# Expert weights loaded four tiles at a time, as runs of 32 KB per partition, in a two-block transformer kernel on one core

## The chip, the cores and the metric

The kernel runs on one core of one Trainium2 chip, with the other seven idle. The metric is the device time of one launch in microseconds (us). All arithmetic is float32 (some operands are split in a high and a low float32r part). Five engines have programs of their own, written out by hand, and meet at semaphores: PE (TensorE, the matrix products), DVE (VectorE), ACT (ScalarE), POOL (GpSimd) and SP (SyncE), which here only issues DMAs.

## The reference

Two blocks over 256 tokens of width 1024. The first block is a gated recurrent mixer followed by a mixture of experts; the second is another mixer with a gated output. The change touches the mixture of experts and, by one term, the router ahead of it:

```
def moe_expert_choice(h, router_w, w_gate, w_up, w_down):
    cap = CAPACITY_FACTOR * T // N_EXPERTS            # 2 * 256 // 16 = 32 tokens for each expert
    aff = softmax(h @ router_w)
    gate, idx = top_k(swapaxes(aff, 1, 2), cap)       # each of the 16 experts picks its 32 tokens
    xs = h[idx]
    hid = silu(xs @ w_gate) * (xs @ w_up)             # w_gate, w_up: 16 x 1024 x 2048
    ye = (hid @ w_down) * gate                        # w_down: 16 x 2048 x 1024
    return zeros.at[idx].add(ye)
```

The three weight tensors are 16 x 3 x 8 MB = 384 MB (MB here is 1024 x 1024 bytes; in the profile's rows it is 1,000,000). They are read once.

## The kernel before

**Tiles.** The expert weights are cut into 24 x 16 = 384 tiles of 1 MB (128 partitions x 8 KB), numbered `t = 0 .. 383`: for each expert `x`, tiles `24x .. 24x+7` are `w_gate` (`wg`), the next eight `w_up` (`wu`), the last eight `w_down` (`wd`). One DMA loads a pair of tiles, `t` and `t+1`, 2 MB: each partition receives one run of 16 KB that is contiguous in HBM (two rows of `wg`/`wu`, or four rows of `wd`). Because partition `p` holds rows `2p, 2p+1`, the activations that meet a tile are gathered with a stride (`H2k[..., k % 2 :: 2]`), and the inner values `hid` are turned by four transposes of `hid[:, c::4]`.

**Buffers.** SBUF is cut into slots of 8 KB per partition. A slot number names a place: 0 to 4 are the five slots of the dense weights (`wslot0` to `wslot4`), 5 and up are the pages of a zone (`zpair(i)` is page `i`), `EXTRA = 25` is a pair of pages of its own (page 17), and `APART = 26` is a mark, not a place: its two tiles go to `wslot4` and to page 15, by two DMAs of 1 MB. The table `PAIRS` gives the place of each pair in order of time. The first ten pairs (`t = 0 .. 19`) fill empty places; the sixth to tenth are issued when the last dense weights free them. From `t = 20` on each pair waits until PE has used the tiles that lay in its place; `before(t)` looks up which tile that is, and SP waits for `p_exp.at("tile", before(t))`. In the steady state nine pairs are in turn, so a pair is asked for when 16 tiles (16 MB) are still outstanding.

**SP's order.** SP issues every weight DMA in the order of the program, and a wait on SP holds back all that stands behind it. Ahead of the experts stand the loads of the first block's dense weights; behind the last expert pair stand those of the second block, `weights(n)`.

**PE's order.** At the end of the first block's dense products come four small products of `ffs` with parts of the identity (line 1918), which bring two vectors into the layout of the gathered activations. Then the output projection, the router, and, interleaved with the products of expert 0, the gathering of activations (`gather_first`, `gather`). `up(x, m, b)` runs the eight tiles of `wg` (m = 0) or `wu` (m = 1): it waits for a pair at every second tile, runs four products per tile (line 2113) and signals `p_exp("tile", t)`. Then `hid` is turned (line 2132, signal `hidT`), and the `wd` tiles follow (line 2147), two per turn of the loop. The last pair, `t = 382`, comes as two DMAs of 1 MB.

Of the kernel before, what the change touches and what calls it, by code (L numbers as in the profile page):

```python
# [64 lines left out]
def program(nc, a, out):  # L65
    ctx = ExitStack()
    with ctx:
# [124 lines left out]
        WH2 = [put(f"whj{i}", 2048, page(p), FR) for i, p in enumerate((14, 15, 6))]  # L192
# [10 lines left out]
        c2, c2l = both("c2", 2048, page(0))  # L203
# [101 lines left out]
        zpair = lambda i: BASE + i  # L305
# [5 lines left out]
        tile_page = lambda t: PAIRS[t // 2]  # L311
        pairs = {r: put(f"pair{r}", 2 * SLOT, page(17) if r == EXTRA else slots_at + r * SLOT if r < BASE else page(r - BASE)) for r in set(PAIRS) - {APART}}
        apart = (slots[4], put("apart", SLOT, page(15)))

        def tile_at_page(t):
            return apart[t % 2] if tile_page(t) == APART else pairs[tile_page(t)][:, t % 2 * SLOT:t % 2 * SLOT + SLOT]

        last_tile = lambda r: max(2 * i + 1 for i in range(12 * NE) if PAIRS[i] == r)
# [6 lines left out]
        def expert_src(t):  # L325
            e_, m, k = t // 24, t % 24 // 8, t % 8
            if m == 2:
                return a["wd"][e_, 256 * k:256 * k + 512, :].rearrange("(p c) n -> p (c n)", c=4)
            return a["wu" if m else "wg"][e_, 128 * k:128 * k + 256, :].rearrange("(p c) n -> p (c n)", c=2)
# [50 lines left out]
        def sync(e):  # L380
# [39 lines left out]
            def experts(t):  # L420
                if tile_page(t) == APART:
                    e.dma_start(apart[0], expert_src(t)[:, 0:SLOT]).then_inc(*landed[APART]())
                    e.dma_start(apart[1], expert_src(t)[:, SLOT:2 * SLOT]).then_inc(*landed[APART]("expert", t))
                    return
                if t == 24 * NE - 2:

                    e.dma_start(pairs[tile_page(t)][:, 0:SLOT], expert_src(t)[:, 0:SLOT]).then_inc(*l_last())
                    e.dma_start(pairs[tile_page(t)][:, SLOT:2 * SLOT], expert_src(t)[:, SLOT:2 * SLOT]).then_inc(*landed[tile_page(t)]("expert", t + 1))
                    return
                e.dma_start(pairs[tile_page(t)], expert_src(t)).then_inc(*landed[tile_page(t)]("expert", t))  # L430
# [31 lines left out]
            for t in range(10, 24 * NE, 2):  # L462
# [11 lines left out]
                elif before(t) is not None:  # L474
                    e.wait_ge(*p_exp.at("tile", before(t)))
                elif tile_page(t) == zpair(12):
                    e.wait_ge(*a_moe.at("xs", 1, 7))
                experts(t)

            for n in range(SECOND, NT):  # L480
                if n < SECOND + 4:
                    e.wait_ge(*p_exp.at("tile", last_tile(tile_slot(n) // 2 * 2)))
                elif n == SECOND + 4:
                    e.wait_ge(*p_exp.at("tile", max(i for i in range(24 * NE) if tile_page(i) == APART)))
# [3 lines left out]
                if n == SECOND + BASE - 1:  # L488
                    e.wait_ge(*p_exp.at("tile", last_tile(zpair(10))))
# [8 lines left out]
        def scalar(e):  # L498
# [220 lines left out]
            for k in range(8):  # L719
                if k == 7:  # L720
                    e.wait_ge(*p_exp.at("tile", 2 * PAIRS.index(EXTRA) + 1))
                    pp_left(0)
# [892 lines left out]
        def gpsimd(e):  # L1615
# [34 lines left out]
            e.wait_ge(*p_exp.at("tile", last_tile(zpair(0))))  # L1650
# [3 lines left out]
        def tensor(e):  # L1654
# [261 lines left out]
            for b_ in range(2):  # L1916
# [501 lines left out]
```

## Time and profile before

| | |
|---|---|
| time, median of 3 runs (lowest, highest) | 1550.55 us (1549.97, 1551.77) |
| time of the profiled execution | 1551.3 us |
| its span in the trace | 1549.5 us |
| granted TensorE clock, mean | 0.89 of full |
| PE busy | 1207.3 us (78%) |
| PE weight loads busy | 730.7 us (47%) |
| DVE / ACT / POOL busy | 562.5 / 423.9 / 29.9 us |
| DMA moved | 520.90 MB, 336 GB/s over the span |

The profiled execution's time is 1.8 us above its span. The page of the profile cuts the span into 40 slices of 38.7 us. The first eight (to about 310 us) are the first block's dense part, the next 23 (to about 1200 us) the experts, the last eight the second block. A "pair" in the rows is a pair of expert tiles, `wslot` a slot of dense weights, `xs` the gathered activations, `B` a bank of PSUM.

### The profile page before, as it was taken

To read this page: it belongs to the slowest core of one execution; us is meant where nothing else is said; L and a number is where in the kernel's file an instruction comes from. 1 tells how busy PE (TensorE), PEld (TensorE's weight loads), DVE (VectorE), ACT (ScalarE), POOL (GpSimd) and SP (SyncE) were. 2 spreads that over 40 slices of the span, in tenths; PEclk is the share of its full clock that TensorE was granted. 3 is DMA by queue.
4 is the path that set the end of the run, shared out by engine and by line. 5 is a ranking of instruction groups with operands and counts; after the bars stand their busy time and mean duration, and the time that the engine had idled before them with its cause. 6 is when DMAs were issued, how large, how long until landed. Compare 5 with 4: busy or idle time off the path is not lost.

```text
span 1549.5 us, 18615 instructions
## 1 busy us (share of the span) xinstructions
PE 1207.3 (78%) x8122; PEld 730.7 (47%) x8122; DVE 562.5 (36%) x829; ACT 423.9 (27%) x553; POOL 29.9 (2%) x36
## 2 busy tenths in 40 slices
PE   4999999999656656656666656656666899999998
PEld 1878899943111212111111111211211589999997
DVE  3887776511101101101101101101101497777566
ACT  2865646232000000000000000000000454467545
POOL 0012000000000000000000000000000000000000
PEclk9999999999778878778867888878778999999999
DMA  9546859699999999999999999999999855555551
GB/s 364 207 156 229 301 209 337 223 403 429 426 428 428 428 428 427 428 428 426 428 428 427 427 428 428 427 427 429 428 427 428 327 164 163 163 183 184 184 186 55
DMA packets 118719, 520.90 MB, mean 336 GB/s; under 512 B 7264, under 2 KB 85088, under 8 KB 90736
## 3 DMA queue, kind: packets, MB, share of 16 engines
q1 hardware_dynamic: 118496, 519.64, 83.9%
q8 instruction: 64, 1.05, 0.3%
q10 hardware_dynamic: 144, 0.09, 0.0%
q14 instruction: 15, 0.12, 0.0%
HBM read 518.66 MB, written 1.05 MB: 335 GB/s over the span
## 4 chain that ended last, share of the span: by engine, by line
DMA 53%; PE 43%; DVE 2%; ACT 1%; SPq 1%; issue 0%; DVEq 0%
DMA pair<-in_wu 27%; PE B L1697 16%; DMA pair<-in_wd 12%; DMA pair<-in_wg 11%; PE B L1705 6%; PE B L2113 4%; PE B L1709 3%; DMA wslot<-in_w_in 2%; PE B L1824 2%; PE B L2147 1%; PE B L1675 1%; PE B L1812 1%; PE B L1827 1%; DMA wslot<-in_w_out 1%; DMA wslot<-in_ada_w 1%; PE B L2074 0%
## 5 line engine op out<-in xcount | busy, mean ns | idle before, releaser
L2113 PE MATMUL B<-pair,xs 128*32 128x512 f32 x2048 | 323.1, 758 | 193.0 <-DMA pair<-in_wu 121.5
L2113 PEld LDWEIGHTS B<-pair,xs 128*32 128x32 f32 x2048 | 63.2, 124 | 413.0 <-issue 180.1
L2147 PE MATMUL B<-pair,hidT 128*32 128x512 f32 x1008 | 167.9, 799 | 102.1 <-DMA pair<-in_wd 96.6
L1697 PE MATMUL B<-hnh,whj 128*128 128x256 f32 x488 | 138.1, 283 | 0.0
L1697 PE MATMUL B<-hnh,wslot_r 128*128 128x256 f32 x488 | 137.6, 282 | 0.0
L1697 PE MATMUL B<-hn_r,whj 128*128 128x256 f32 x488 | 137.1, 281 | 0.0
L2147 PEld LDWEIGHTS B<-pair,hidT 128*32 128x32 f32 x1008 | 32.3, 128 | 218.6 <-DMA pair<-in_wd 143.2
L955 DVE TENSOR_TENSOR wslot_r<-wslot,whj 128x2048 fp32r<-128x2048 f32 x52 | 118.9, 2289 | 31.3 <-ACT whj L509 31.3
L509 ACT ACTIVATE whj<-wslot 128x2048 fp32r<-128x2048 f32 x51 | 97.2, 1913 | 87.6 <-PE B L1697 82.0
L1289 DVE SCALAR_TENSOR_TENSOR x<-B,mod,x 128x256 f32<-128x256 f32 x128 | 56.0, 480 | 163.5 <-PE B L2092 163.3
L1320 DVE COPY ye<-B 128x512 f32<-128x512 f32 x15 | 10.4, 692 | 269.6 <-PE B L2147 269.6
L1309 DVE TENSOR_TENSOR hid<-sgm,B 128x512 f32<-128x512 f32 x16 | 11.0, 688 | 260.8 <-PE B L2113 260.8
L1697 PEld LDWEIGHTS B<-hnh,wslot_r 128*128 128x128 f32 x488 | 93.6, 192 | 0.0
L1697 PEld LDWEIGHTS B<-hn_r,whj 128*128 128x128 f32 x488 | 91.8, 188 | 0.1
L1697 PEld LDWEIGHTS B<-hnh,whj 128*128 128x128 f32 x488 | 91.7, 188 | 0.1
L736 ACT ACTIVATE hidT<-B 128x512 f32<-128x512 f32 x16 | 9.6, 597 | 271.1 <-PE B L2132 271.1
L730 ACT ACTIVATE gt<-B 128x256 f32<-128x256 f32 x16 | 6.1, 383 | 273.4 <-PE B L2124 273.4
L745 ACT ACTIVATE ye<-B 128x512 f32<-128x512 f32 x15 | 9.0, 597 | 247.7 <-PE B L2147 247.7
L955 DVE TENSOR_TENSOR wslot_r<-wslot,whi 128x2048 fp32r<-128x2048 f32 x29 | 66.3, 2286 | 13.0 <-ACT whi L509 10.7
L1705 PE MATMUL B<-hh,whi 128*128 128x256 f32 (+1 forms) x256 | 71.0, 308 | 0.0
L1705 PE MATMUL B<-h_r,whi 128*128 128x256 f32 (+1 forms) x256 | 69.6, 303 | 0.0
L2092 PE MATMUL B<-gt,ye 128*128 128x256 f32 x256 | 68.4, 413 | 1.5
(505 smaller groups left out, 1908.8 us busy)
## 6 DMA issues: line engine op xcount, KB each, us to landing
pair<-in_wg SPq DMA_DIRECT2D x64, 2048.0 KB, 41.2
pair<-in_wu SPq DMA_DIRECT2D x64, 2048.0 KB, 40.9
pair<-in_wd SPq DMA_DIRECT2D x62, 2048.0 KB, 40.9
wslot<-in_w_in SPq DMA_DIRECT2D x58, 1024.0 KB, 5.2
aslot<-in_ada_w SPq DMA_DIRECT2D x20, 1024.0 KB, 7.2
wslot<-in_ada_w SPq DMA_DIRECT2D x4, 1024.0 KB, 9.1
wslot<-in_w_out SPq DMA_DIRECT2D x4, 1024.0 KB, 8.5
wslot<-in_wa SPq DMA_DIRECT2D x4, 1024.0 KB, 5.1
```

Source lines behind the costliest of these rows:

```text
L509: e.activation(hi_(n), raw(n), ACT.Copy).then_inc(*a_hi(n))
L955: e.tensor_tensor(lo_(n), raw(n), hi_(n).bitcast(F32), ALU.subtract).then_inc(*v_lo(n))
L1289: e.scalar_tensor_tensor(XX[:, db, :], B[scat_bank(x, db // 2)][:, 256 * (db % 2):256 * (db % 2) + 256], mod[:, 40 + db, 0:1], XX[:, db, : ...
L1675: mm = e.matmul(B[0][32 * j:32 * j + 32, :], csil[:, k, :], slots[s][:, 512 * j:512 * j + 512], start=k == 0, stop=k == 7)
L1697: mm = e.matmul(ps, w[:, k, :], x(k), start=k == 0 and j == 0, stop=k == kn - 1 and j == 2)
L1705: e.matmul(ps, l, r, start=k == 0 and j == 0, stop=False)
L1709: mm = e.matmul(ps, l, r, start=False, stop=k == kn - 1)
L1812: mm = e.matmul(B[4 + j][:, half(h)], K0[:, h, half(j)], Q0[:, h, half(i)], start=True, stop=True)
L1824: e.matmul(ps, x[:, 4 * half_k + k, tk], wh[:, k, :], start=half_k == 0 and k == 0 and x is ah, stop=False)
L2092: mm = e.matmul(B[b][:, 256 * j:256 * j + 256], YE[:, half(db)], Gt, start=True, stop=True)
L2113: mm = e.matmul(B[b][32 * j:32 * j + 32, :], XS[x // 8][:, k, 32 * (x % 8):32 * (x % 8) + 32], tile_at_page(t)[:, 512 * j:512 * j + 512], ...
L2147: mm = e.matmul(B[3 + db][32 * r:32 * r + 32, :], hidT[:, 128 * c + 32 * j:128 * c + 32 * j + 32], v2(tile_at_page(t + c // 2))[:, c % 2, ...
```

## The change

- From `t = 28` on, four tiles are loaded by one DMA of 4 MB: each partition receives one run of 32 KB contiguous in HBM. There are 88 such loads (`t = 28 .. 379`), in turn over four places: slots 0 to 3, and pages 8, 0 and 4 of the zone (each four pages wide).
- The first 14 loads stay pairs, in the same places as before, and the last two (`t = 380`, `382`) are pairs too. A pair is now half of a run of 32 KB, so partition `p` holds rows `4p .. 4p+3` of `wg`/`wu`, or `8p .. 8p+7` of `wd`, spread over four tiles. The gathering strides become 4 in place of 2 (same number of products).
- `hid` is turned by sixteen products with parts of the identity (64 columns each) in place of four transposes; the products of `ffs` become 16 in place of 4.
- The table is now `LOADS`, a list of (first tile, number of tiles, place). `before(load)` now looks for earlier loads whose slots, counted as `place .. place + number - 1`, overlap those of the load.
- The third high-part buffer of the second block (`WH2`) and the buffer `c2` exchange pages 6 and 0.

The core of the diff:

```
-        TURN = [zpair(2), zpair(4), zpair(12), zpair(0), zpair(6), 0, 2, zpair(8), zpair(10)]
         EXTRA = BASE + MORE + AUX
         APART = EXTRA + 1
-        PAIRS = TURN[:2] + [EXTRA] + TURN[3:] + [APART] + 2 * (TURN[:2] + TURN[3:])
-        PAIRS += [TURN[i % 9] for i in range(12 * NE - len(PAIRS))]
+        LOADS = [(2 * i, 2, r) for i, r in enumerate((zone_at(2), zone_at(4), EXTRA, zone_at(0), zone_at(6), 0, 2, zone_at(8), zone_at(10), APART,
+                                                      zone_at(2), zone_at(4), zone_at(0), zone_at(6)))]
+        for t in range(28, 24 * NE, 4):
+            r = zone_at(8) if t == 24 * NE - 4 else (0, zone_at(8), zone_at(0), zone_at(4))[(t - 28) // 4 % 4]
+            LOADS += [(t, 2, r), (t + 2, 2, r + 2)] if t == 24 * NE - 4 else [(t, 4, r)]
...
-        def before(t):
-
-            earlier = [i for i in range(t // 2) if PAIRS[i] == PAIRS[t // 2]]
-            return 2 * earlier[-1] + 1 if earlier else None
+        in_slot = lambda s, load: load[2] <= s < load[2] + load[1]
+        def before(load):
+
+            t0, n, r = load
+            earlier = [x[0] + x[1] - 1 for x in LOADS if x[0] < t0 and any(in_slot(s, x) for s in range(r, r + n))]
+            return max(earlier) if earlier else None
...
-            for t in range(10, 24 * NE, 2):
+            for load in LOADS[5:]:
+                t = load[0]
...
-                elif before(t) is not None:
-                    e.wait_ge(*p_exp.at("tile", before(t)))
-                elif tile_page(t) == zpair(12):
-                    e.wait_ge(*a_moe.at("xs", 1, 7))
+                elif before(load) is not None:
+                    e.wait_ge(*p_exp.at("tile", before(load)))
                 experts(t)
...
-            for b_ in range(2):
-                for hf in range(2):
-                    mm = e.matmul(B[4][64 * hf:64 * hf + 64, 0:16].rearrange("p (m q b) -> p b m q", m=2, b=2)[:, b_], ident[:, b_::2],
-                                  ffs.rearrange("p (m q h) -> p h m q", m=2, h=2)[:, hf], start=True, stop=True)
+            for b_ in range(4):
+                for hf in range(4):
+                    mm = e.matmul(B[4][32 * hf:32 * hf + 32, 0:16].rearrange("p (m q b) -> p b m q", m=2, b=4)[:, b_], ident[:, b_::4],
+                                  ffs.rearrange("p (m q h) -> p h m q", m=2, h=4)[:, hf], start=True, stop=True)
...
-                for c in range(4):
-                    mm = e.transpose(B[2][:, half(c)], hid[:, c::4], ident)
+                for c in range(8):
+                    for q in range(2):
+                        mm = e.matmul(B[2][64 * q:64 * q + 64, 64 * c:64 * c + 64].rearrange("p (j s) -> p j s", j=2), hid[:, c::8],
+                                      ident.rearrange("p (j q s) -> p q j s", q=2, s=32)[:, q], start=True, stop=True)
```

**SP at the start of the experts, before.** The rows are SP's DMAs in order: `pair_198` holds `t = 12`, `pair_203` `t = 14`, `pair_204` `t = 16`; `wslot_57` and `apart` together hold `t = 18` and `19` (the APART load); then `t = 20, 22, 24, 26, 28, 30`.

```order
73 L430 DMA pair_198<-in_wu 128x4096 [waits pe_proj]
74 L430 DMA pair_203<-in_wu 128x4096 [waits pe_proj]
75 L430 DMA pair_204<-in_wd 128x4096
76 L422 DMA wslot_57<-in_wd 128x2048
77 L423 DMA apart<-in_wd 128x2048
78 L430 DMA pair_200<-in_wd 128x4096 [waits pe_expert]
79 L430 DMA pair_201<-in_wd 128x4096 [waits pe_expert]
80 L430 DMA pair_199<-in_wg 128x4096 [waits pe_expert]
81 L430 DMA pair_202<-in_wg 128x4096 [waits pe_expert]
82 L430 DMA pair_197<-in_wg 128x4096 [waits pe_expert]
83 L430 DMA pair_198<-in_wg 128x4096 [waits pe_expert]
```

**The same place of SP in the changed kernel.** Row 82 is the first load of four tiles (`t = 28`).

```order
73 L443 DMA pair_203<-in_wu 128x4096 [waits pe_proj]
74 L443 DMA pair_298<-in_wu 128x4096 [waits pe_proj]
75 L443 DMA pair_299<-in_wd 128x4096
76 L435 DMA wslot_57<-in_wd 128x2048 [waits pe_expert]
77 L436 DMA apart<-in_wd 128x2048
78 L443 DMA pair_206<-in_wd 128x4096 [waits pe_expert]
79 L443 DMA pair_207<-in_wd 128x4096 [waits pe_expert]
80 L443 DMA pair_208<-in_wg 128x4096 [waits pe_expert]
81 L443 DMA pair_209<-in_wg 128x4096 [waits pe_expert]
82 L443 DMA four_294<-in_wg 128x8192 [waits pe_expert]
83 L443 DMA four_295<-in_wu 128x8192 [waits pe_expert]
```

No load has moved in the order, but the first DMA of the APART load (row 76) has gained a wait for a tile that PE has used, and from row 82 on one DMA stands where two stood. By the new `before`, the APART load has place 26 and two slots, 26 and 27; the EXTRA load (`t = 4`) has place 25 and two slots, 25 and 26; they overlap at 26, so the wait is for tile 5.

**PE ahead of the output projection, before.** `ffs` is the small vector pair, `hh` and `bf_r` are operands of dense products.

```order
935 L1709 MATMUL B<-hh,wslot_r 128x256 x7
936 L1918 MATMUL B<-ffs,ident 64x8 [waits dve_mid,dve_left_bank]
937 L1918 MATMUL B<-ffs,ident 64x8 x3
938 L1923 MATMUL B<-wrbsum,ones 128x16 [waits dve_left_bank]
939 L1705 MATMUL B<-bf_r,whi_98 128x256 [waits act_hi,dve_clamped,dve_h]
```

**The same place of PE in the changed kernel.**

```order
935 L1721 MATMUL B<-hh,wslot_r 128x256 x7
936 L1930 MATMUL B<-ffs,ident 32x4 [waits dve_mid,dve_left_bank]
937 L1930 MATMUL B<-ffs,ident 32x4 x15
938 L1935 MATMUL B<-wrbsum,ones 128x16 [waits dve_left_bank]
939 L1717 MATMUL B<-bf_r,whi_98 128x256 [waits act_hi,dve_clamped,dve_h]
```

Twelve small products are added in front of the projections. The turning of `hid` grows in the same way, from four products of 128x128 to sixteen of 64x64 for each expert, at the same place of PE's order.

## Rows read from the trace of the kernel before

**Rows 1.** The page: the span in 40 slices, DMA share, GB/s and PE's clock.

```profile
PEclk9999999999778878778867888878778999999999
DMA  9546859699999999999999999999999855555551
GB/s 364 207 156 229 301 209 337 223 403 429 426 428 428 428 428 427 428 428 426 428 428 427 427 428 428 427 427 429 428 427 428 327 164 163 163 183 184 184 186 55
```

**Rows 2.** The page: the chain that ended last, by line.

```profile
DMA pair<-in_wu 27%; PE B L1697 16%; DMA pair<-in_wd 12%; DMA pair<-in_wg 11%; PE B L1705 6%; PE B L2113 4%; PE B L1709 3%; DMA wslot<-in_w_in 2%; PE B L1824 2%; PE B L2147 1%; PE B L1675 1%; PE B L1812 1%; PE B L1827 1%; DMA wslot<-in_w_ou
```

**Rows 3.** Waits of PE from 400 to 1180 us: total us, times, longest.

```profile
PE B L2113 <- DMA pair<-in_wu: 113.0, 52, 3.1
PE B L2147 <- DMA pair<-in_wd: 88.4, 46, 3.0
PE B L2113 <- DMA pair<-in_wg: 66.2, 35, 3.2
```

**Rows 4.** DMA queues from 420 to 1180 us: packets, MB, share of 16 engines.

```profile
DMA packets 22324, 325.10 MB, mean 428 GB/s; under 512 B 2480, under 2 KB 2480, under 8 KB 2480
q1 hardware_dynamic: 22298, 324.71, 100.5%
q8 instruction: 22, 0.36, 0.2%
pair<-in_wu SPq DMA_DIRECT2D x52, 2048.0 KB, 41.3
```

**Rows 5.** DMA queues from 1300 to 1500 us (the second block's dense weights).

```profile
DMA packets 35507, 36.04 MB, mean 180 GB/s; under 512 B 544, under 2 KB 35490, under 8 KB 35490
q1 hardware_dynamic: 35490, 35.79, 56.2%
wslot<-in_w_in SPq DMA_DIRECT2D x20, 1024.0 KB, 5.2
```

**Rows 6.** SP's issues in order of time, from 300 us: start, us, what.

```profile
303.34 0.43 SPq L430 DMA_DIRECT2D pair<-in_wd  x1
303.81 0.43 SPq L422 DMA_DIRECT2D wslot<-in_wd  x1
304.29 0.74 SPq L423 DMA_DIRECT2D apart<-in_wd  x1
318.36 4.53 SPq L430 DMA_DIRECT2D pair<-in_wd  x2
329.19 12.24 SPq L430 DMA_DIRECT2D pair<-in_wg  x4
```

**Rows 7.** DMA issues at 304.29 and at 329.19: KB, us to landing.

```profile
apart<-in_wd SPq DMA_DIRECT2D x1, 1024.0 KB, 17.7
pair<-in_wg SPq DMA_DIRECT2D x1, 2048.0 KB, 10.1
```

**Rows 8.** PE in order of time from 315 us: tiles 0, 1, 5.

```profile
315.65 1.07 PE L2113 MATMUL B<-pair,xs 128*32 128x512 f32 x8
...
317.23 1.06 PE L2113 MATMUL B<-pair,xs 128*32 128x512 f32 x8
...
325.62 1.07 PE L2113 MATMUL B<-pair,xs 128*32 128x512 f32 x8
```

**Rows 9.** Windows in us: busy time of PE, PEld, DVE, ACT, POOL, PEclk, DMA share, GB/s.

```profile
318.00:320.00 2.00, 2.00 (x18) 0.93 (x14) 0.00 (x0) 0.38 (x1) 0.00 (x0) 1.00 0.87 369
320.00:322.00 2.00, 2.00 (x18) 0.93 (x14) 0.00 (x0) 0.38 (x1) 0.00 (x0) 1.00 0.95 352
330.00:332.00 2.00, 2.00 (x14) 0.85 (x12) 0.00 (x0) 1.94 (x4) 0.20 (x1) 1.00 0.93 303
332.00:334.00 2.00, 2.00 (x14) 0.85 (x12) 0.69 (x1) 0.83 (x2) 0.00 (x0) 1.00 0.92 303
```

**Rows 10.** PE in order of time from 250.5 us.

```profile
250.63 0.41 PE L1918 MATMUL B<-ffs,ident 128*64 128x8 f32 x8
250.98 0.39 PE L1923 MATMUL B<-wrbsum,ones 128*128 128x16 f32 x2
```

More of the change, by code:

```diff
@@ L189, in program @@
         gkh_ = put("gkh", 128, lbv_at + 128, FR)
-        WH2 = [put(f"whj{i}", 2048, page(p), FR) for i, p in enumerate((14, 15, 6))]
+        WH2 = [put(f"whj{i}", 2048, page(p), FR) for i, p in enumerate((14, 15, 0))]
         YH, YL = v8(put("yh", 2048, page(7), FR)), v8(put("yl", 2048, page(8), FR))
@@ L202, in program @@
         hn, hnl = both("hn", 2048, page(13))
-        c2, c2l = both("c2", 2048, page(0))
+        c2, c2l = both("c2", 2048, page(6))
         PT2, mg2l = both("PT2", 2048, page(1))
@@ L313, in program @@
+        load_of = {t: load for load in LOADS for t in range(load[0], load[0] + load[1])}
+        tile_page = lambda t: load_of[t][2]
+        homes = {(n, r): put(("pair" if n == 2 else "four") + str(r), n * SLOT, page(17) if r == EXTRA else slots_at + r * SLOT if r < BASE else page(r - BASE))
+                 for _, n, r in LOADS if r != APART}
         apart = (slots[4], put("apart", SLOT, page(15)))
         def tile_at_page(t):
-            return apart[t % 2] if tile_page(t) == APART else pairs[tile_page(t)][:, t % 2 * SLOT:t % 2 * SLOT + SLOT]
@@ L318, in program, with last_tile @@
-        last_tile = lambda r: max(2 * i + 1 for i in range(12 * NE) if PAIRS[i] == r)
-        def before(t):
-            earlier = [i for i in range(t // 2) if PAIRS[i] == PAIRS[t // 2]]
-            return 2 * earlier[-1] + 1 if earlier else None
-        def expert_src(t):
+            t0, n, r = load_of[t]
+            return apart[t - t0] if r == APART else homes[n, r][:, (t - t0) * SLOT:(t - t0 + 1) * SLOT]
+        in_slot = lambda s, load: load[2] <= s < load[2] + load[1]
+        def last_tile(s):
+            return max(load[0] + load[1] - 1 for load in LOADS if in_slot(s, load))
@@ L420, in experts @@
             def experts(t):
-                if tile_page(t) == APART:
-                    e.dma_start(apart[0], expert_src(t)[:, 0:SLOT]).then_inc(*landed[APART]())
-                    e.dma_start(apart[1], expert_src(t)[:, SLOT:2 * SLOT]).then_inc(*landed[APART]("expert", t))
+                n, r = load_of[t][1:]
+                if r == APART:
+                    e.dma_start(apart[0], expert_src(t, 2)[:, 0:SLOT]).then_inc(*landed[APART]())
+                    e.dma_start(apart[1], expert_src(t, 2)[:, SLOT:2 * SLOT]).then_inc(*landed[APART]("expert", t))
                     return
                 if t == 24 * NE - 2:
-                    e.dma_start(pairs[tile_page(t)][:, 0:SLOT], expert_src(t)[:, 0:SLOT]).then_inc(*l_last())
-                    e.dma_start(pairs[tile_page(t)][:, SLOT:2 * SLOT], expert_src(t)[:, SLOT:2 * SLOT]).then_inc(*landed[tile_page(t)]("expert", t + 1))
+                    e.dma_start(homes[n, r][:, 0:SLOT], expert_src(t, 2)[:, 0:SLOT]).then_inc(*l_last())
+                    e.dma_start(homes[n, r][:, SLOT:2 * SLOT], expert_src(t, 2)[:, SLOT:2 * SLOT]).then_inc(*landed[r]("expert", t + 1))
                     return
-                e.dma_start(pairs[tile_page(t)], expert_src(t)).then_inc(*landed[tile_page(t)]("expert", t))
+                e.dma_start(homes[n, r], expert_src(t, n)).then_inc(*landed[r]("expert", t))
             def later(j):
@@ L481, in sync @@
                 if n < SECOND + 4:
-                    e.wait_ge(*p_exp.at("tile", last_tile(tile_slot(n) // 2 * 2)))
+                    e.wait_ge(*p_exp.at("tile", last_tile(tile_slot(n))))
                 elif n == SECOND + 4:
-                    e.wait_ge(*p_exp.at("tile", max(i for i in range(24 * NE) if tile_page(i) == APART)))
+                    e.wait_ge(*p_exp.at("tile", last_tile(APART)))
                 else:
@@ L488, in sync @@
                 if n == SECOND + BASE - 1:
-                    e.wait_ge(*p_exp.at("tile", last_tile(zpair(10))))
+                    e.wait_ge(*p_exp.at("tile", last_tile(zone_at(11))))
                     e.dma_start(wgk[0:16, :], a["w_gk2"]).then_inc(*l_gk())
@@ L720, in scalar @@
                 if k == 7:
-                    e.wait_ge(*p_exp.at("tile", 2 * PAIRS.index(EXTRA) + 1))
+                    e.wait_ge(*p_exp.at("tile", last_tile(EXTRA)))
                     pp_left(0)
```

24 lines of the change are left out of this document (13 added, 11 removed).

## Prediction

> **What bounds the kernel now.** I read the 40 slices of the page first. From about 350 to 1200 us every slice has a DMA share of 9 tenths or more and 426 to 429 GB/s, while PE's granted clock falls to 0.7 to 0.8 [rows 1]: in this stretch TensorE stands at its lower level (1.2 GHz) for part of the time and at 2.4 GHz for the rest, because it has too little to do. The chain of work that ended last gives half of the span to the three weight tensors (27 + 12 + 11%) [rows 2]. PE's waits say the same from the other side: between 400 and 1180 us PE waits 113.0 + 88.4 + 66.2 = 267.6 us for expert tiles [rows 3]. So the expert stage ends when its 384 MB have come through the DMA queues. Two things can move that end: how fast the stream runs, and how long it stands still. Work of PE counts only where a load waits for it.
>
> **The stream: what a longer run is worth.** At 428 GB/s [rows 4] a pair of 2,097,152 bytes takes 4.900 us. Each of the 16 DMA engines carries 8 runs of 16 KB and one small packet for the semaphore in that time. How much of it goes with the packet and not with the bytes? The queue view of this stretch has 22,298 - 2,480 = 19,818 large packets; 100.5% of 16 engines for 760 us is 12,221 us, so 616.7 ns each [rows 4]. The second block has 35,490 - 544 = 34,946 packets of 1 KB in 56.2% of 16 x 200 us, so 51.5 ns each [rows 5]. Between 1 KB and 16 KB a KB costs (616.7 - 51.5) / 15 = 37.7 ns. The bytes of a pair therefore take 8 x 16 x 37.7 ns = 4.823 us. Of the 4.900 us some 0.005 us are instruction loads (0.36 of 325.1 MB [rows 4]), and 0.072 us are left that come once per DMA of 8 runs, whatever their length. A load of four tiles pays them once for 4 MB: 9.72 us in place of 9.79. Over the 88 loads that is 88 x 0.072 = 6.3 us saved. The bounds: the intercept of a small packet is 51.5 - 37.7 = 13.8 ns, which over 8 x 88 = 704 packets fewer per engine makes 9.7 us; and nothing, if a run of 32 KB goes out as two packets. I take 6.3, since it comes from the rate of this very stretch. The trace has no packet of 32 KB, so all of this is an estimate from the rows at 1 and 16 KB.
>
> The Trainium skill, "DMA: Bandwidth & Descriptors", section "Why small descriptors are slow", puts the cost inside an engine at about 3 cycles per packet, next to one cycle for every 32 bytes. By it a packet's own part would be some 3.5 ns and the saving 2.5 us; the rows give 0.072 / 8 = 9 ns, so the trace does not agree, though it has no run of 32 KB to decide it. That is a rival below.
>
> **The stream: a hole at its start.** The listing of SP shows the term that weighs most. In the changed kernel the first DMA of the APART load (t = 18) waits for PE to finish tile 5. The place of this load needs no such wait: EXTRA (25, two slots) and APART (26, a mark) overlap only by their numbers. Before, t = 16, 18 and 19 were issued at 303.34, 303.81 and 304.29 us, one right behind the other [rows 6], and tile 19 landed 17.7 us later, at 322.0 [rows 7]; as its 4.9 us of data end there, those of t = 18 began at 317.1. At 318.36, when tile 1 was done, t = 20 followed, and the stream hardly broke [rows 6, 9]. Tile 5 is done only at 325.62 + 1.07 = 326.7 us [rows 8]. SP is in order, so t = 20, 22, 24 stand behind the waiting load although tiles 1 and 3 are long used.
>
> PE itself arrives a little later. The four products of ffs take 0.35 us from their start to the next product's (250.63 to 250.98) [rows 10]; sixteen take, by the same 0.09 us, 1.4 us, some of it a fixed drain. PE has hardly a gap there, so I add 0.8 us (bounds 0 and 1.05). Tile 5 then ends at 327.5, and the load is issued at 327.55. From issue to first data: a tile of 1 MB with 1 KB runs lands after 5.2 us, of which 64 packets x 51.5 ns = 3.3 us are data [rows 5], so about 2.0 us with its completion. The data of t = 18 start at about 329.55 in place of 317.1: 12.5 us later. Between, nothing is in the queue.
>
> Not all of this reaches the end, for the stream of before also had small dips: at 318 to 322 us (369 and 352 GB/s) and at 330 to 334 (303 twice) [rows 9] it lost 0.3 + 0.4 + 1.2 = 1.8 us against 428. With loads asked for in time behind the hole these vanish, which leaves 10.7. Measured at a later load: t = 24 landed at 329.19 + 10.1 = 339.3 [rows 6, 7]; now it lands four pairs behind 329.55, at 349.15, 9.9 us later, but a landing is set by the slowest of 16 engines, and a hole lets all start level. I take 11.6, the middle of 10.7 and 12.5; the bounds are 9.9 and 12.5.
>
> Behind the hole nothing else is late. PE needs (325.62 - 317.23) / 4 = 2.1 us per tile here [rows 8], so tile 13, for which the first load of four (t = 28) waits, is done near 344, while the pairs up to t = 26 keep the queue full until 354. Tile 17 (for t = 32) is done near 353, before t = 28 ends at 364; tile 25 near 370, before t = 32 ends at 374. In the steady state a load of four is asked for when 12 tiles are outstanding in place of 16, so 29 us of data in place of 39 (before, a pair landed 41.3 us after its issue [rows 4]). PE would have to be more than 27 us behind for the queue to run dry, and it is the one that waits.
>
> **What costs nothing.** The turning of hid: twelve more small products per expert, at the 0.09 us of those of ffs [rows 10] 1.1 us each time, up to double at the lower clock. The waits of PE for tiles (267.6 us) [rows 3] hide them; if that cover were gone they would cost 17 us or more. The gathering keeps its number of products. At the end of the stage the last tiles come as pair, single, single, as before; the dense weights behind them have the same places. The wait of wgk for tile 383 stands behind dense tiles that are issued later than that tile's use. The exchanged pages 6 and 0 are both free by then.
>
> **Sum.** 11.6 (hole, with the 0.8 of PE in it) - 6.3 (88 loads) = +5.3 us. Against the profiled execution's 1551.3 us that is 1556.6. The median of the three runs is 0.75 us lower, 1550.55, so I predict 1555.9 us. A measurement of this kernel can tell about 0.2%, 3.1 us, from no change.
>
> **The rivals.**
> - *The two nearly cancel.* A packet costs nearly the 13.8 ns of the intercept (9 us saved) and the hole costs its lower bound (9.9 to 11): 10.9 - 8.9 = +2, 1552.6 us. For it: the intercept itself; against it: the rate of the stretch leaves no room for 13.8 ns. 0.16.
> - *The longer run gives back little.* By the 3 cycles of the page above: 11.6 - 2.5 = +9.1, 1559.7 us. The 9 ns from the rate speak against it, the lack of any row at 32 KB for it. 0.09.
> - *The run is cut into packets of 16 KB.* Then only the hole is left: +11.6, 1562.2 us. The runs of 16 KB went out whole (19,818 packets carry the bytes of as many runs [rows 4]), which speaks against. 0.05.
> - *The loads of four run slower*, from how 16 engines spread over HBM when a partition's rows lie 32 KB apart, or from a queue that runs dry. Each per cent on 88 x 9.8 us is 8.6 us: 1551.3 + 11.6 + 8.6 - 0.7 = 1570.8. It takes over from the forecast once a load of four takes more than 9.79 us. 0.04.
> - *Faster than before.* A long run moves its bytes faster than 37.7 ns per KB, so that the stream gives back more than the hole: it needs 11.6 + 3.1 = 14.7 us, 0.167 us per load, a load of four in under 9.63 us (436 GB/s). At 438 GB/s a load takes 9.58 us, 88 x 0.21 = 18.5 us are saved, and the time is 1550.55 + 11.6 - 18.5 = 1543.7 us. No slice of the page's long stretch is over 429. 0.07.
>
> **How the numbers follow.** The forecast has 0.59, with a range of its own of 1553.7 to 1558.7 (hole 10.7 to 12.5, saving 4.4 to 7.5). Slower by over 0.2%: forecast, little given back, cut, slower loads, 0.59 + 0.09 + 0.05 + 0.04 = 0.77. Within 0.2%: 0.16. Faster: 0.07. The range of 1551.5 to 1562.0 takes in the forecast, most of the near-cancelling case, and the case of little given back; it leaves out the faster case and the two slowest.
>
> **What the profile of the changed kernel would show.** If the hole is right: SP's issue of t = 18 right behind tile 5, near 327.5 us, with t = 20 and 22 within 1 us behind it, and windows of 0 GB/s between about 317 and 329 us. If the price of a packet is right: packets of 32 KB, 88 x 128 = 11,264 fewer in all, and 431 GB/s in the long stretch. At 429 the page's 3 cycles hold; at 428 or below the runs are cut or slowed. Waits of PE for hid's turning should not appear on the chain that ended last. The prediction is wrong above all if the hole is shorter (tile 5 earlier, or the queue still full), or if the stream's rate moves by more than 1%.

## The result, and the profile of the changed kernel

The changed kernel takes 1558.93 us in the median (1557.54 to 1560.2, 4 runs), the kernel before in the same series 1551.12 (1549.97 to 1551.77, 4 runs). The ratio is 1.0051, with a 95% interval of 1.0034 to 1.0068: slower by 7.8 us, between 5.3 and 10.5. The profiled execution took 1558.16 us with a span of 1556.4, against 1551.3 and 1549.5 before, 6.9 us more. The granted clock is 0.895 in the mean.

The page of the changed kernel, its 40 slices (the span is 1556.4 us, a slice 38.9):

```profile
PEclk9999999999888788878878787877797999999999
DMA  9646768659999999999999999999999855455551
GB/s 363 217 156 232 284 231 331 233 240 432 432 431 433 431 432 430 430 431 432 430 431 430 431 432 430 432 431 431 431 432 430 331 168 171 155 183 185 184 188 55
```

Against [rows 1] two things have changed. The ninth slice, 311 to 350 us, has fallen from 403 to 240 GB/s. The long stretch behind it has risen from 426 to 429 up to 430 to 433. These are the two terms of the prediction: a hole, and a faster stream.

**The hole.** SP's DMAs in order of time, changed kernel, from 302 us (start, us, what):

```profile
302.67 0.43 SPq L443 DMA_DIRECT2D pair<-in_wd  x1
329.16 0.33 SPq L435 DMA_DIRECT2D wslot<-in_wd  x1
329.53 0.43 SPq L436 DMA_DIRECT2D apart<-in_wd  x1
330.35 1.02 SPq L443 DMA_DIRECT2D pair<-in_wd  x2
332.07 4.91 SPq L443 DMA_DIRECT2D pair<-in_wg  x2
345.48 0.33 SPq L443 DMA_DIRECT2D four<-in_wg  x1
```

The APART load (`t = 18`) stands 26.5 us behind `t = 16`, where it stood 0.5 us behind it [rows 6]. With it go `t = 20` and `22` (the row with 1.02 us), `t = 24` and `26` (4.91 us). Windows of the changed kernel (columns as in [rows 9]):

```profile
314.00:316.00 2.00, 2.00 (x13) 1.86 (x16) 0.48 (x2) 0.52 (x2) 0.00 (x0) 1.00 0.00 0
316.00:328.00 12.00, 12.00 (x68) 6.57 (x60) 0.00 (x0) 2.12 (x6) 0.00 (x0) 1.00 0.01 1
328.00:330.00 2.00, 2.00 (x13) 1.13 (x12) 0.00 (x0) 0.60 (x2) 0.62 (x1) 1.00 0.00 0
330.00:332.00 2.00, 2.00 (x18) 0.52 (x19) 0.00 (x0) 1.81 (x4) 0.00 (x0) 1.00 0.94 262
332.00:352.00 20.00, 19.12 (x121) 10.74 (x120) 2.06 (x3) 6.59 (x13) 0.62 (x1) 1.00 1.01 431
```

For 16 us, from 314 to 330, nothing moves. PE is busy the whole time: it works on what it has, and the queue is empty beside it. The first DMA behind the hole and `t = 24`, from issue to landing (KB, us):

```profile
wslot<-in_wd SPq DMA_DIRECT2D x1, 1024.0 KB, 4.8
pair<-in_wg SPq DMA_DIRECT2D x1, 2048.0 KB, 20.5
```

`t = 24` lands at 332.07 + 20.5 = 352.6, before at 339.3 [rows 6, 7]: 13.2 us later. Why the wait lasts to 329.1 and not to 327.5 stands in PE's order of time, around tile 0, tile 1 and tile 5:

```profile
315.75 1.07 PE L2125 MATMUL B<-pair,xs 128*32 128x512 f32 x8
316.75 1.12 PE L2076 MATMUL B<-pick,h2k 128*128 128x32 f32 x4
317.80 1.06 PE L2125 MATMUL B<-pair,xs 128*32 128x512 f32 x8
...
328.04 1.06 PE L2125 MATMUL B<-pair,xs 128*32 128x512 f32 x8
```

Tile 0 starts 0.1 us later than before, tile 5 2.4 us later. From tile 1 on a tile takes (328.04 - 317.80) / 4 = 2.56 us in place of 2.1 [rows 8]. Between two tiles stand the products that gather activations. Grouped by line and form (busy us, mean ns), they read their weights (`H2k`, a step of four floats) so:

```profile
L2086 PEld LDWEIGHTS B<-pick,h2k 128*128 128x128 f32 x64 | 16.4, 325 | 12.6 <-ACT xs L725 9.2 <-issue 3.2
L2076 PEld LDWEIGHTS B<-pick,h2k 128*128 128x128 f32 x32 | 8.0, 325 | 5.0 <-issue 3.4 <-ACT xs L720 1.7
```

Before, with a step of two floats, the second of these groups read:

```profile
L2064 PEld LDWEIGHTS B<-pick,h2k 128*128 128x128 f32 x32 | 4.3, 196 | 5.0 <-issue 3.4 <-ACT xs L708 1.7
```

The same number of products, but 325 ns for each weight load in place of 196: four of them between two tiles are 0.52 us, about the difference of the pace.

**The stream.** Queues of the changed kernel from 420 to 1180 us (packets, MB, share of 16 engines):

```profile
DMA packets 11257, 327.51 MB, mean 431 GB/s; under 512 B 1248, under 2 KB 1248, under 8 KB 1248
q1 hardware_dynamic: 11230, 327.10, 100.1%
```

The runs of 32 KB went out whole: 11,230 - 1,248 = 9,982 large packets in 100.1% of 16 x 760 us, 1.219 us each, where two of 16 KB took 1.233 [rows 4]. A load of four, 4,194,304 bytes, takes 9.73 us at 431 GB/s and 9.80 at 428: 0.07 us on each of 88, or 6.0 us. The rounding of either rate alone is worth up to 1 us there. With the rates unrounded (327.51 and 325.10 MB in 760 us) the two loads take 9.733 and 9.805 us, and the 88 give 6.3 us.

At the end of the stage, PE's rows of the last `wd` tiles:

```profile
1217.20 5.34 PE L2162 MATMUL B<-four,hidT 128*32 128x512 f32 x32 [1.44 <-DMA four<-in_wd]
1223.56 1.92 PE L2162 MATMUL B<-pair,hidT 128*32 128x512 f32 x16
1226.50 1.92 PE L2162 MATMUL B<-pair,hidT 128*32 128x512 f32 x16
```

The last tile lands at 1226.99 us in the trace, and landed at 1220.42 before: 6.6 us later, so of the 13.2 at `t = 24` the stream has given back 6.6 by then, about what its rate says. The last 0.3 us of the 6.9 arise behind it: PE comes to the last pair at 1226.50 us and runs all its 16 products after that, while before it had run the first eight already when the last tile landed, and had only this row left:

```profile
1220.47 1.07 PE L2147 MATMUL B<-pair,hidT 128*32 128x512 f32 x8 [1.14 <-DMA pair<-in_wd]
```

**Turning `hid`.** The turning before and now, grouped by form:

```profile
L2132 PE MATMUL B<-ident,hid 128*128 128x128 f32 x64 | 12.3, 317 | 14.1 <-DVE hid L1309 14.1
```

```profile
L2145 PE MATMUL B<-ident,hid 128*64 128x64 f32 x512 | 34.5, 287 | 14.2 <-DVE hid L1321 14.2
```

34.5 us busy for 12.3. No sign of it reaches the end: PE still waits for tiles between 400 and 1180 us (total us, times, longest), 266.9 us in all for 267.6 before [rows 3]:

```profile
PE B L2125 <- DMA four<-in_wu: 121.8, 26, 5.8
PE B L2162 <- DMA four<-in_wd: 87.9, 22, 7.3
PE B L2125 <- DMA four<-in_wg: 57.2, 20, 6.3
```

### The profile page after: what moved, and what is told of

Its sections match the earlier page's. It is cut to its first block, busy times and chain, and to the rows that moved or that the text cites. A ratio compares the mean times of both kernels' runs of the same rounds, so it can differ in the third digit from the quotient of the medians.

```text
span 1556.4 us, 19468 instructions
## 1 busy us (share of the span) xinstructions
PE 1216.9 (78%) x8594; PEld 779.3 (50%) x8594; DVE 562.3 (36%) x829; ACT 424.1 (27%) x553; POOL 29.8 (2%) x36
## 4 chain that ended last, share of the span: by engine, by line
DMA 48%; PE 48%; DVE 2%; ACT 1%; SPq 1%; issue 1%; DVEq 0%
DMA four<-in_wu 17%; PE B L1709 16%; DMA four<-in_wd 15%; DMA four<-in_wg 15%; PE B L2125 7%; PE B L1717 6%; PE B L1721 3%; PE B L2162 3%; PE B L1836 2%; PE B L1687 1%; PE B L1824 1%; PE B L1839 1%; PE B L2086 1%; DMA wslot<-in_w_out 1%; DMA wslot<-in_ada_w 1%
## 5 line engine op out<-in xcount | busy, mean ns | idle before, releaser
L2125 PE MATMUL B<-four,xs 128*32 128x512 f32 x1888 | 304.3, 800 | 197.3 <-DMA four<-in_wu 135.4
L2125 PEld LDWEIGHTS B<-four,xs 128*32 128x32 f32 x1888 | 75.3, 140 | 401.5 <-issue 323.9
L2162 PE MATMUL B<-four,hidT 128*32 128x512 f32 x928 | 142.5, 769 | 93.5 <-DMA four<-in_wd 89.3
L2162 PEld LDWEIGHTS B<-four,hidT 128*32 128x32 f32 x928 | 35.2, 136 | 188.6 <-DMA four<-in_wd 87.2
L967 DVE TENSOR_TENSOR wslot_r<-wslot,whi 128x2048 fp32r<-128x2048 f32 x29 | 66.2, 2284 | 12.9 <-ACT whi L521 10.5
L2104 PE MATMUL B<-gt,ye 128*128 128x256 f32 x256 | 63.4, 391 | 1.6
## 6 DMA issues: line engine op xcount, KB each, us to landing
pair<-in_wg SPq DMA_DIRECT2D x6, 2048.0 KB, 11.6
```

The source lines that it names most:

```text
L967: e.tensor_tensor(lo_(n), raw(n), hi_(n).bitcast(F32), ALU.subtract).then_inc(*v_lo(n))
L2104: mm = e.matmul(B[b][:, 256 * j:256 * j + 256], YE[:, half(db)], Gt, start=True, stop=True)
L2125: mm = e.matmul(B[b][32 * j:32 * j + 32, :], XS[x // 8][:, k, 32 * (x % 8):32 * (x % 8) + 32], tile_at_page(t)[:, 512 * j:512 * j + 512], ...
L2162: mm = e.matmul(B[3 + db][32 * r:32 * r + 32, :], hidT[:, 256 * (j % 2) + 64 * c + 32 * (j // 2):256 * (j % 2) + 64 * c + 32 * (j // 2) + 32],
```

## Experiments

Theory after the result: three terms. The wait of `t = 18` costs the hole; the gathering's longer weight loads put PE behind, which lengthens the wait; the cost of a packet comes back on 88 loads. Rivals: that the hole alone explains the loss; that the cost falls once per DMA and not once per packet; that loads of four cost something by themselves.

The median of the kernel before was 1551.06 us in the series of the first four runs below, 1551.37 in that of the next four, and 1551.2 in that of the last two. Each run is compared with the one of its own series.

### The APART load gets a number of its own

```
-        APART = EXTRA + 1
+        APART = EXTRA + 2
-        landed = [signal(f"landed{i}", 16) for i in range(BASE + MORE + AUX + 2)]
+        landed = [signal(f"landed{i}", 16) for i in range(BASE + MORE + AUX + 3)]
```

> The changed kernel with the APART load given a number of its own, so that it waits for no tile. Theory: the wait for tile 5 made the hole of 13 us (stream of t = 18 from 331.0 instead of 317.1 us), and PE's pace of 2.56 us per tile (2.1 before; weight reads of the gathering 325 ns instead of 196) asks for t = 20, 24 and t = 28 too late. Then the dry times move to these: about 1.5 us before t = 20, 3.4 before t = 24, 3.6 before t = 28, the first load of four lands near 357 instead of 365.3 (first engine), and the kernel is about 8 us faster than the changed one: 1551 us, even with before. Rival A: PE's pace does not matter; then only the hole goes, 13 us faster, 1546 us. Rival B: the loss lies in the later stage; then the time stays near 1559 us.

Measured: 1553.79 us (1549.73 to 1556.29, 10 runs), ratio 1.0016 [1.0005, 1.0026]. That is 2.7 us above the kernel before, in place of 7.8. So 5.1 us of the loss go with the wait, less than the hole that could be read in the trace and less than the 8 that were expected. SP issues `t = 18` right behind `t = 16` again, but now other holes appear. SP's issues and windows of this run:

```profile
319.63 6.84 SPq L443 DMA_DIRECT2D pair<-in_wd  x2
334.16 4.91 SPq L443 DMA_DIRECT2D pair<-in_wg  x2
347.57 0.33 SPq L443 DMA_DIRECT2D four<-in_wg  x1
```

```profile
318.00:320.00 2.00, 2.00 (x11) 0.51 (x3) 0.00 (x0) 0.12 (x1) 0.00 (x0) 0.50 0.22 90
320.00:322.00 2.00, 2.00 (x9) 1.13 (x13) 0.00 (x0) 0.38 (x1) 0.00 (x0) 0.50 0.69 180
332.00:334.00 2.00, 2.00 (x18) 0.55 (x17) 0.00 (x0) 1.71 (x4) 0.00 (x0) 1.00 0.25 107
346.00:348.00 2.00, 2.00 (x13) 0.96 (x13) 0.00 (x0) 0.54 (x1) 0.00 (x0) 1.00 0.02 8
```

`t = 24` is issued at 334.16, 5.0 us later than before [rows 6]. The queue runs dry before `t = 20`, before `t = 24` and before the first load of four, because PE is late with the tiles that they wait for. In the changed kernel these waits were hidden in the large hole. Part of the lateness in this run is the clock: 0.50, the level of 1.2 GHz, between 318 and 322 us. How much of the 2.7 us is the clock's, the run doesn't tell: its ten times go from 1549.73 to 1556.29 us, and the traced one, 1555.09, is among the longer ones.

### The kernel before, with the wait alone

```
+                elif t == 18:
+                    e.wait_ge(*p_exp.at("tile", 5))
```

> The kernel before with one wait added: the load of t = 18 waits for tile 5. Theory: t = 18 is issued near 326.8 us, its data start near 328.8 instead of 317.1, the dips at 320 and 330 us go; t = 26 lands 9.5 to 11 us later than before, and the kernel takes 1561 us. Rival: the stream makes the hole good later (a stage that is not bound by DMA), then under 1554 us.

Measured: 1561.03 us (1559.66 to 1561.78, 4 runs), ratio 1.0065 [1.0048, 1.0082]. The wait alone costs 10.0 us by the medians and 10.5 by the spans of the two traces (1560.0 and 1549.5), inside the 9.9 to 12.5 of the prediction and in its lower part. SP issues `t = 18` as soon as tile 5 is done, and the stream stands from about 316 us on:

```profile
326.27 0.33 SPq L422 DMA_DIRECT2D wslot<-in_wd  x1
```

```profile
316.00:326.00 10.00, 10.00 (x72) 4.42 (x68) 0.00 (x0) 1.89 (x5) 0.61 (x1) 1.00 0.01 2
```

That is 2.9 us earlier than in the changed kernel. The rest of that kernel's hole is not the wait's.

### Each four as two DMAs of 16 KB runs

On top of the own number:

```
+                if n == 4:
+                    e.dma_start(homes[n, r][:, 0:2 * SLOT], expert_src(t, 4)[:, 0:2 * SLOT]).then_inc(*landed[r]())
+                    e.dma_start(homes[n, r][:, 2 * SLOT:4 * SLOT], expert_src(t, 4)[:, 2 * SLOT:4 * SLOT]).then_inc(*landed[r]("expert", t))
+                    return
```

> As e1, but each load of four goes out as two DMAs of 2 MB with runs of 16 KB, one right behind the other, same places and waits. Theory (a cost of 8 to 9 ns once per packet): 428 GB/s again in the long stretch, 0.07 us more per load of four, 6 us slower than e1: 1557 us. Rival (the rate comes from fewer waits or from the addresses, not from the run): 431 GB/s and the time of e1.

Measured: 1558.82 us (1556.95 to 1563.25, 4 runs), ratio 1.0058 [1.0039, 1.0077], 5.0 us above the run with the own number. The time alone proves little, since the clock fell in this run's trace too (0.50 from 320 to 328 us, in the longest of its four executions); the rate of the long stretch is the evidence. The queues, 420 to 1180 us:

```profile
DMA packets 22323, 325.05 MB, mean 428 GB/s; under 512 B 2482, under 2 KB 2482, under 8 KB 2482
```

Everything but the length of the run and the number of DMAs is as it was, and the rate is back at 428. So neither the layout nor the places nor the waits of the loads of four make the stream fast; the length of the run or the smaller number of DMAs does.

### Each four as two DMAs of 64 partitions

To keep the 32 KB runs and double the DMAs, each four was cut by partitions:

```
+                    e.dma_start(homes[n, r][0:64, :], expert_src(t, 4)[0:64, :]).then_inc(*landed[r]())
+                    e.dma_start(homes[n, r][64:128, :], expert_src(t, 4)[64:128, :]).then_inc(*landed[r]("expert", t))
```

> As e1, but each load of four goes out as two DMAs, partitions 0 to 63 and 64 to 127, with runs of 32 KB. The number of DMAs doubles as in e3, the packets stay at 32 KB. Theory (cost per packet, a semaphore packet about 9 ns): at most 1 us slower than e1, 430.5 to 431 GB/s. Rival (cost per DMA): 6 us slower, 428 GB/s, as e3.

Measured: 2447.26 us (2445.01 to 2449.91, 4 runs), ratio 1.5785 [1.5761, 1.5808]. The queues, 420 to 1180 us:

```profile
DMA packets 6097, 159.70 MB, mean 210 GB/s; under 512 B 1216, under 2 KB 1216, under 8 KB 1216
q1 hardware_dynamic: 6083, 159.49, 100.2%
```

The experiment doesn't answer its question. It shows something else: (6,083 - 1,216) = 4,867 packets of 32 KB in 100.2% of 16 engines are 2.50 us each, twice as long as for 128 partitions, with all 16 engines occupied. The Trainium skill, "SBUF — State Buffer", section "Door 1: The DMA port swizzle", says that the partitions 0 to 63 reach only half of SBUF's 16 ports, 218 GB/s at most; the trace agrees, with 210.

### The kernel before, with the longer step in the gathering

```
-  H2k[:, i, 256 * (k // 2) + k % 2:256 * (k // 2) + 256:2]
+  H2k[:, i, 512 * (k // 4) + k % 4:512 * (k // 4) + 512:4]
```

> The kernel before with one change: the gathering products read their weights from H2k with a step of 4 floats (16 bytes) instead of 2, as the changed kernel does. The weights of the experts stay in the old layout, so features and weight rows no longer belong together and the values of the expert part differ; the work is the same. Theory (a step of 16 bytes makes the weight read slower): weight loads of the gathering 325 ns instead of 196, 2.5 us per tile at the start instead of 2.1, tile 5 near 329 instead of 326.7 us; the stream runs dry longer before t = 24 and the kernel is 2 to 4 us slower than before. Rival (the slower pace in the changed kernel came with the hole or the runs): 196 ns and the time of before.

Measured: 1556.18 us (1552.5 to 1557.83, 10 runs), ratio 1.0029 [1.002, 1.0038], so 4.8 us by the medians for the step alone, above the 2 to 4 that were expected. The weight load takes what it took in the changed kernel:

```profile
L2064 PEld LDWEIGHTS B<-pick,h2k 128*128 128x128 f32 x32 | 8.0, 325 | 5.0 <-issue 3.4 <-ACT xs L708 1.7
```

No DMA, wait or place was touched. The pace of the changed kernel comes with it: in the trace tile 1 starts at 317.15 us and tile 5 at 327.39, so 2.56 us per tile, and SP issues `t = 24` at 331.42 where it stood at 329.19 [rows 6]. The clock is 1.00 there:

```profile
318.00:322.00 4.00, 4.00 (x24) 2.62 (x20) 0.00 (x0) 0.51 (x2) 0.00 (x0) 1.00 0.77 250
```

This traced execution took 1553.08 us, only 1.8 more than that of the kernel before; the ten times go from 1552.5 to 1557.83. So the trace holds 1.8 of the 4.8 us, and the rest lies in executions without a trace. A fall of the clock, as in the traces of the two runs above that read with this step and have no hole, is a candidate for it and is not shown.

### The changed kernel, with `H2k` written in the order of its reading

ACT now permutes while it writes, and PE reads 128 contiguous floats. The hole stays.

```
+  e.activation(H2k[:, i, 512 * c:512 * c + 512].rearrange("p (r m) -> p m r", r=4), B[2 * c + i].rearrange("p (m r) -> p m r", r=4), ...
+  e.matmul(B[b][:, 0:32], H2k[:, i, 128 * k:128 * k + 128], Pm[:, i, 0, :], ...
```

> The changed kernel, hole included, with H2k written by ACT in the order in which the gathering reads it, so that its weight reads are contiguous. Theory: weight loads near 190 ns, tile 5 near 326.5 instead of 329.1 us, the load of t = 18 is issued by as much earlier, and the kernel is 2 to 2.5 us faster than the changed one: 1556.5 us. The strided write by ACT may take back some tenths. Rival (PE's pace is set by other waits): 1558.9 us.

Measured: 1555.49 us (1555.01 to 1556.75, 7 runs), ratio 1.0028 [1.0018, 1.0039], by the distances to the kernel before 3.7 us less than the changed kernel (4.1 for 7.8), where 2 to 2.5 were expected. The rows: PE's weight load, SP's issue of `t = 18`, ACT's writing of `H2k`.

```profile
L2076 PEld LDWEIGHTS B<-pick,h2k 128*128 128x128 f32 x32 | 4.1, 190 | 5.0 <-issue 3.4 <-ACT xs L720 1.7
```

```profile
326.25 0.33 SPq L435 DMA_DIRECT2D wslot<-in_wd  x1
```

```profile
L716 ACT ACTIVATE h2k<-B,rsc 128x512 f32<-128x512 f32 x4 | 3.8, 1112 | 0.0
```

With the reads back at 190 ns the issue of `t = 18` is back at 326.25, where the wait alone had put it (326.27). So the changed kernel's hole is made of two parts that add: the wait, up to 326.3, and PE's lateness of 2.9 us. ACT pays for the permuted writing with 1112 ns for 684, and once PE waits for it: 0.89 us in front of a product of line 2048, a wait that the traces of the kernel before and of the changed kernel don't have.

### Both: own number and packed `H2k`

> Both mended: the APART load with its own number and H2k packed. Theory: the stream hardly breaks at the start, except for at most 1 us before t = 28 (tile 13 done near 341 to 342 us), and the 88 long runs give their 6.2 us: 1546 us, 0.3% faster than before. Rival (waiting for tile 13 in place of tile 11 starves the stream by more): 1549 us or more.

The two edits above together. Measured: 1548.09 us (1545.69 to 1549.77, 11 runs), ratio 0.9977 [0.9968, 0.9986]: faster than the kernel before by 3.3 us, 2.1 us longer than expected and 1.7 us short of what the terms give (below). Two windows show where the queue still runs short:

```profile
318.00:320.00 2.00, 2.00 (x15) 0.83 (x15) 0.00 (x0) 0.38 (x1) 0.00 (x0) 1.00 0.70 176
342.00:344.00 2.00, 2.00 (x20) 0.83 (x12) 0.00 (x0) 0.59 (x2) 0.00 (x0) 1.00 0.86 344
```

### The old layout, each four as one DMA with runs of 16 KB

The kernel before with the new table of loads, the own number, and the old strides and transposes. A load of four gives each partition two runs of 16 KB:

```
+  return a["wu" if m else "wg"][e_, 128 * k:128 * k + 128 * n, :].rearrange("(h p c) n -> p h (c n)", h=n // 2, c=2)
```

> The old layout of the weights (gathering with step 2, four transposes of hid), the APART load with its own number, and loads of four as one DMA whose partitions get two runs of 16 KB each: 44 DMAs per engine's 8 x 88 = 704 packets fewer do not exist, only the number of DMAs is that of the changed kernel. Theory (cost per packet): 428 GB/s, packets of 16 KB, the time within 1.5 us of before, 1551 to 1552.5 us. Rival (cost per DMA): 431 GB/s and 1546 us.

The number of DMAs is here that of the changed kernel, but its 704 fewer packets per engine are not. Measured: 1552.7 us (1551.13 to 1554.82, 10 runs), ratio 1.0011 [1.0002, 1.0021]. The queues, 420 to 1180 us:

```profile
DMA packets 21093, 325.14 MB, mean 428 GB/s; under 512 B 1247, under 2 KB 1247, under 8 KB 1247
```

The small packets are as few as in the changed kernel (1,247), the large ones as many as before, and the rate is 428. Half the DMAs gave nothing: the cost goes with the large packet. That is the question the cut by partitions had left open. And without its long runs the new table costs 1.3 us by the medians, with an interval of 0.3 to 3.3, just outside nothing. That loads of four ask for their place later and end the stage in coarser pieces may be the reason; it is not shown, and the traced execution is only 0.5 us above that of the kernel before (1551.78 and 1551.3).

### The kernel before, with runs of 8 KB

Each pair as two DMAs of one tile each:

```
+  e.dma_start(pairs[tile_page(t)][:, 0:SLOT], expert_src(t)[:, 0:SLOT]).then_inc(*landed[tile_page(t)]())
+  e.dma_start(pairs[tile_page(t)][:, SLOT:2 * SLOT], expert_src(t)[:, SLOT:2 * SLOT]).then_inc(...)
```

> The kernel before with each pair loaded as two DMAs of 1 MB, runs of 8 KB per partition: twice the packets. Theory (8 to 9 ns once per packet): a pair takes 4.97 instead of 4.90 us, 422 GB/s in the long stretch, and the 182 pairs behind the start make the kernel 12 to 13 us slower than before: 1564 us. Rival (a packet's cost is hidden below the bytes for runs of 8 KB and more, and only 32 KB differ): 428 GB/s and 1551 us.

Measured: 1564.45 us (1563.42 to 1565.06, 4 runs), ratio 1.0084 [1.007, 1.0098], 13.2 us more. The queues, 420 to 1180 us:

```profile
DMA packets 43942, 320.18 MB, mean 421 GB/s; under 512 B 4881, under 2 KB 4881, under 8 KB 4881
```

A third point. 4 MB take 9.96 us at 421 GB/s, 9.80 at 428 and 9.73 at 431; an engine carries 32, 16 and 8 runs in that time. From 32 to 16 the difference is 0.16 us or 10 ns a packet, from 16 to 8 it is 0.07 us or 9 ns (to 1 or 2 ns, by the rounding of the rates). The medians say the same: 13.2 us over 192 pairs with 8 more packets per engine are 8.6 ns each.

### Pairs up to `t = 31`, fours from `t = 32`

The last version with both edits, and the loads of `t = 28` and `30` left as pairs in slots 0 and 2:

```
-        for t in range(28, 24 * NE, 4):
+        for t in range(32, 24 * NE, 4):
```

> As e7, with t = 28 and t = 30 still loaded as pairs, the first load of four being t = 32. Theory: t = 28 is asked for at tile 11 instead of 13, about 4 us earlier, the dip before it goes, and the kernel is up to 1 us faster than e7: 1547.2 us. Rival (the slowest DMA engine was late anyway, so the dip costs nothing): 1548.1 us, as e7. The difference may lie within what the measurement can tell.

Measured: 1546.92 us (1545.43 to 1548.48, 6 runs), ratio 0.9969 [0.9957, 0.9982]. The window that was short is full:

```profile
342.00:344.00 2.00, 2.00 (x16) 0.83 (x12) 0.00 (x0) 0.59 (x2) 0.00 (x0) 1.00 1.09 459
```

By the medians that is 1.0 us better than the run before it (4.3 us below the kernel before, for 3.3); the intervals overlap, so the gain of this step is not shown. The version as a whole is the fastest here, 2.8 to 6.7 us below the kernel before.

## Why the prediction was right where it was, and where it was not

**The number.** 1558.93 us lies in the stated range of 1551.5 to 1562.0, and 0.2 us above the 1553.7 to 1558.7 that the forecast gave to its own sum. The rise is 7.8 us where 5.3 were forecast. By the number alone the rival of 1559.7 (little given back) would have been the better one; it is the stream's rate and the later runs that speak for the forecast's two terms.

**What bounds the kernel.** Right. The stage ended when its last tiles had landed, and PE's waits for tiles stayed at 267 us.

**What a longer run is worth (6.3 us, from 9 ns per packet).** Right in size and in mechanism. The stream went to 431 GB/s as forecast for that price; runs of 8 and 16 KB in other kernels gave 421 and 428, on one line; and one DMA of two short runs gave nothing. The rivals of the 3 cycles, of the cut packets and of the slower loads of four have fallen. So has the one by which the two terms nearly cancel through 13.8 ns a packet. Its figure was not wrong as a packet's time: two packets of 16 KB take 2 x 616.7 ns and one of 32 KB 1219, 14 ns less. But the times of 16 KB packets add up to 100.5% of the stretch and those of 32 KB to 100.1%, so packets overlap a little, and the rate keeps only 9 of the 14 ns. The Trainium skill, "DMA: Bandwidth & Descriptors", section "Why small descriptors are slow", has about 3 cycles per packet; the trace doesn't agree, the cost is some 2.7 times that at every length tried.

**The hole (11.6 us, with 0.8 of PE in it).** The mechanism was right: a wait that only the numbering asks for, SP's order that holds `t = 20` to `24` behind it, and a queue that runs dry for 16 us. The size was a little too large for the wait by itself: 11.6 less the 0.8 of PE is 10.8, and it costs 10.0 to 10.5 us in the old kernel. The deduction of the small dips was right to make. The hole of the changed kernel as it stands, with PE's lateness in it, lies above the bound of 12.5: `t = 24` landed 13.2 us later.

**PE's delay by the products of `ffs` (0.8 us).** This term was mis-sized. Changed kernel, PE in order of time:

```profile
249.81 0.66 PE L1930 MATMUL B<-ffs,ident 128*32 128x4 f32 x32
250.41 0.39 PE L1935 MATMUL B<-wrbsum,ones 128*128 128x16 f32 x2
```

Sixteen products take 0.60 us to the next one's start where four took 0.35 [rows 10]. The 0.09 us per product were mostly a fixed part of the group; the added twelve cost 0.25 us together.

**"The gathering keeps its number of products" (0 us).** This is the step that failed. The number is the same and the read is not: with a step of 16 bytes a weight load takes 325 ns for 196. PE was 2.4 us later at tile 5 than in the profile of before, and SP's wait ended 2.9 us later than with the wait alone. In the kernel before the step alone costs 1.8 us in the traced execution and 4.8 in the median, and packing `H2k` takes 3.7 us from the changed kernel. I had counted instructions and priced the edit by the count, though the diff changes the access pattern of each.

**Nothing else is late behind the hole.** Right for the changed kernel (431 GB/s in the window behind it). Taken out of that kernel it would be wrong: with the wait gone and the slow reads left, the queue ran dry in front of `t = 20`, `24` and `28`, in a trace with the clock at its lower level for a part of it. The hole covered the lateness.

**Turning `hid` (0 us).** Right as far as the runs show: 22 us more of PE, and its waits for tiles are as long as before. No run has it alone.

**The sum.** Prediction: 11.6 - 6.3 = 5.3. Runs: 10.0 (wait) + 2.9 (issue of `t = 18` later through the reads) - 6.3 (stream) + 0.3 (end of the stage) = 6.9, which is the difference of the two spans. That it fits to the tenth is luck: each term is sure to some tenths only, with the wait's 10.5 by the spans the sum is 7.4, and the medians differ by 7.8. The total came near because two errors of opposite sign, the hole 1.1 to 1.6 too large with its `ffs` part and the reads 2.9 too small, partly met; that too is luck.

**What stays open.** With both faults mended, the terms give 1551.37 + 1.3 (the new table, measured with short runs) - 6.3 = 1546.4 us; 1548.09 was measured. The traced execution of that kernel took 1546.41, so the 1.7 us lie between it and the median, where no trace is. ACT's slower writes of `H2k` make PE wait 0.89 us once in this trace, and still tile 0 starts at 315.36 us, 0.3 before that of the kernel before, and SP issues `t = 24` at 328.74 for 329.19; that they cost the kernel anything is not shown. Which part of the 1.3 us belongs to the later asking and which to the end of the stage was not separated. And the part of the clock in the times of the runs with slow reads and no hole stays open.

## What to carry to other kernels

Where a change makes runs longer by giving a partition other rows, price every reader of the data by its new step and not by its number of instructions: packing what PE's weight loads read took 3.7 us off the changed kernel, more than half of the 6.3 that the stream won. When a rule computes waits from slot numbers, list each load that has gained a wait, and read from the trace how long the queue can go on without it: this one had data for about 12 us, from 302 to 314, and the wait took 26. And when a hole is mended, look behind it, since it hides every lateness that is smaller than itself.

## What the runs showed of the hardware

- **Weight loads and steps.** 128x128 float32 weights, mean of a group: 189 to 196 ns contiguous, 196 at a step of 8 bytes, 325 at 16 bytes. The Trainium skill, "SBUF — State Buffer", has 16-byte cachelines in its section on the port swizzle and asks for at least two hits in each; with 8 bytes there are two, with 16 one, and the trace agrees. Its remark there that one can stride four float32 for free doesn't hold for these loads.
- **ACT's writing with a step.** 128x512 float32 from PSUM: 684 ns contiguous, 1112 ns with neighbouring elements 512 bytes apart.
- **Half of the partitions, half of the rate.** 210 GB/s for DMAs of 64 partitions with the other half next in the queue, and 2.50 us for a packet of 32 KB in place of 1.22. The engines show as fully busy the whole time, so the share of busy engines alone tells nothing of the rate.
- **Price of a packet.** 9 to 10 ns of the stream's time between runs of 8, 16 and 32 KB, and nothing that the rate shows for a DMA as such (428 GB/s with one DMA for 4 MB or two, at runs of 16 KB).
- **A fall of the clock in the busy start.** In the run with the own number the granted clock was 0.50 (1.2 GHz) from 318 to 324 us and 1.00 from 314 to 317 and again from 325, with PE busy for 2.00 of every 2.00 us from 314 us on, before the fall and in it. In the run with halved runs it was 0.50 from 320 to 328 us. The traces of all other runs show 1.00 between 314 and 332 us. Three kernels with the step of four floats and no hole have the widest spreads of those near 1550 us (1549.73 to 1556.29, 1556.95 to 1563.25 and 1552.5 to 1557.83), but the trace of the third shows 1.00. That the clock makes the spread is a guess: one trace of each was taken.
